# Weight splits moved up behind the joints, residual updates put ahead of them, two modulation tiles moved, and one scan matrix for both directions, in a two-layer hybrid trunk

## The chip, the cores and the metric

The kernel runs on one core of a Trainium2 chip (trn2). The metric is the device time of one execution in microseconds. The profile shows five engines: PE (TensorE, with its weight loads as PEld), DVE (VectorE), ACT (ScalarE), POOL (GpSimd) and SP (SyncE, which here only issues the weight transfers).

## What is computed

Two layers run over 384 tokens (256 latent, 128 context) with a model width of 1024, all in fp32. Cut to what matters here:

```python
h = rmsnorm(x, g1) * (1 + sc1) + sh1          # sc, sh, g: x @ w_mod rows of silu(c), silu(c_ctx)
u, q, k, v, z, xbc, dt_raw = split(h @ w_in)
o_pool = multiscale_pool_mixer(u)             # windows 2, 4, 8, 16
o_att  = diff_attention(rope(q), rope(k), v)  # 4 heads, two softmax maps each
xbc = silu(dwconv3(xbc)); dt = softplus(dt_raw + bias); a = -exp(A_log)
# per chunk of 128 tokens, head h, direction d (forward and backward):
#   y += (C B^T * exp(segsum_d) * dt_d) x  +  C (state_d * exp(cumsum_d))
o_ssd = rmsnorm_grouped((y_f + y_b + D * x) * silu(z))
merged = sum(sigmoid(h @ w_gate) * (o @ w_branch)) over the three branches
x = x + g1 * (merged @ w_out)
h2 = rmsnorm(x, g2) * (1 + sc2) + sh2
up = dwconv3(h2 @ w_up); x = x + g2 * ((silu(up_gate) * up_val) @ w_down)
```

The outputs are the two token streams after a last norm, the new keys and values, and the final scan states.

## The kernel before

**Units.** All dense products run as a list of units (`UNITS`), 140 to a layer, in this order: XBC 8, U 4, Q 4, K 4, V 4, Z 4, GATE 24, BRANCH 12, OUT 8, UP 44, DOWN 24. A unit is one 128x1024 block of weights (896 columns for some of DOWN). Its product is taken in three fp32r parts (high by high, high by low, low by high), so a unit is 24 matmuls of 128x384. Activations lie transposed, channels on partitions and tokens in the free dimension.

**Splits.** Weights come from HBM by SP into `raw` (4 slots). ACT copies the high part into `wh` (function `hi`, L1158), DVE takes the low part `wl` (function `lo`, L1511). Both have three slots, so unit u+3 can be split only when PE has finished unit u. The function `ahead(l, u)` of ACT and of DVE issues the split of unit u+3. In the loop over the units each engine does, for unit u: the bank's evacuation or taps, then `ahead`, then the rest (`conv_result`, `update` and others).

**Joints.** After each norm the first three units (XBC 0 to 2, or UP 0 to 2) run together (`joint`): for each of the eight tiles k of the normed input, PE multiplies with all three weight blocks as soon as `hh` and `hl` of that tile are there. For tiles 6 and 7 it waits for the last low part and then runs unit by unit.

**XBC and UP units.** They carry a depthwise convolution: ACT evacuates the bank with the middle tap (L1279), DVE adds the two outer taps in four instructions (L1661), ACT takes a tanh (L1317), DVE multiplies (`conv_result`, L1672, L1676, L1682). After each pair of UP units ACT and DVE write the product's high and low part (`ah` L1175, `al` L1516).

**OUT and DOWN units.** DVE adds the result to `x` (`update`, L1723), ACT squares the new `x` into `th` (L1261), POOL sums six of the squares into `sqa`. After the last unit, PE sums over channels (`mean_squares`, L774 to L778: first `sqa`, then the squares of tiles 6 and 7), ACT makes 1/rms, and the next norm begins.

**Modulation tiles.** The adaLN rows are computed on DVE beside the units, one tile of 128 weight rows at a place (`modulation`, L1586, two instructions of 128x1024). `mod_places` sets the places: in each layer every unit from U 0 to V 3 (`FRONT`), eight units of GATE, and every fifth of UP. Q 0 and K 0 also hold a rotation (L1691 to L1694).

**The scan** runs beside GATE and BRANCH, in six steps (chunk c of 3, group g of 2), one every two units. PE broadcasts the exponents (`rows`, L1056), DVE adds the column's part `nac` and a mask for each direction and head (`decays`, L1785), ACT takes the exponent (L1399, L1400), DVE multiplies by dt and by B^T C (`matrices`, L1796) and scales the entering states' factors `eb` (L1800), PE multiplies (`scan_out`, L1078). An fp32 matmul shows as two records.

## Time and profile before

| | |
|---|---|
| median of 3 runs | 1368.4 us (1368.32 to 1369.77) |
| the profiled execution's own time | 1367.94 us |
| its span, first to last instruction | 1366.2 us |
| PE busy | 1308.7 us, 96% |
| DVE busy | 1095.0 us, 80% |
| ACT busy | 647.9 us, 47% |
| POOL busy | 162.3 us, 12% |

Busy time of PE is the union of matmul records, whose ends are modelled; two records of neighbouring matmuls overlap. So for PE the distance between starts tells more than the busy share. A value in square brackets is idle time just before an instruction, with what ended it.

### The profile page before, as it was taken

The page shows a single profiled execution, that of the slowest core. Times are in us where ns is not written, and L with a number is a line of the kernel's source. Part 1 is how long each engine was busy: PE and PEld are TensorE (multiplying, and loading weights), DVE is VectorE, ACT ScalarE, POOL GpSimd, SP SyncE. Part 2 cuts the span into 40 slices and gives each one's busy share as a digit, 9 for nine tenths or more (in the row PEclk, how much of TensorE's full clock was granted, in tenths as well). Part 3 has the DMA queues.
Part 4 walks back from the last instruction along what each step waited for, and adds up shares of the span by engine and source line. Part 5 has one row for each costly group of instructions (what it writes and reads, how often), then busy time and mean ns, then how long its engine had stood idle before and what let it go on. Part 6 is the DMA issues. An engine that isn't in the chain of part 4 may idle for free.

```text
span 1366.2 us, 20140 instructions
## 1 busy us (share of the span) xinstructions
PE 1308.7 (96%) x7564; PEld 1245.6 (91%) x7564; DVE 1095.0 (80%) x2104; ACT 647.9 (47%) x1037; POOL 162.3 (12%) x167
## 2 busy tenths in 40 slices
PE   5899999999998999999999999999999899999996
PEld 4799889999997999999989978899999799999996
DVE  5889988779857999999958998877876689999432
ACT  4643445644546445442355335545455654454331
POOL 0058000000310000000102910000031000000001
PEclk8999999999999999999999999999999999999998
DMA  9466525433343444457725672552234254444441
GB/s 365 144 204 211 199 96 205 141 101 95 116 145 106 140 156 155 139 185 259 245 85 171 215 232 77 185 186 94 92 108 148 83 167 154 140 158 133 142 127 47
DMA packets 58433, 210.00 MB, mean 154 GB/s; under 512 B 6752, under 2 KB 8928, under 8 KB 56800
## 3 DMA queue, kind: packets, MB, share of 16 engines
q1 hardware_dynamic: 55648, 197.53, 43.6%
q0 software_dynamic: 2688, 11.18, 2.4%
q8 instruction: 60, 0.98, 0.3%
q14 instruction: 37, 0.30, 0.1%
HBM read 205.01 MB, written 3.67 MB: 153 GB/s over the span
## 4 chain that ended last, share of the span: by engine, by line
PE 60%; DVE 26%; ACT 7%; issue 5%; DMA 1%; POOL 0%; SPq 0%; ACTq 0%; DVEq 0%; POOLq 0%
PE acc L826 17%; PE acc L827 17%; PE acc L828 17%; DVE wl L1511 6%; DVE junk_front L1586 5%; DVE cv L1661 3%; ACT wh L1158 1%; DVE gates L1705 1%; PE mix L1078 1%; DVE ee L1796 1%; DVE ee L1785 1%; PE mix L983 1%; DMA head<-in_whead_dram 1%; DVE hl L1516 1%; DVE x L1723 1%
## 5 line engine op out<-in xcount | busy, mean ns | idle before, releaser
L826 PE MATMUL acc<-hh,wh 128*128 128x384 f32 x1528 | 522.2, 342 | 7.5 <-DVE wl L1511 5.3
L828 PE MATMUL acc<-hh,wl 128*128 128x384 f32 x1528 | 511.1, 334 | 0.0
L827 PE MATMUL acc<-hl,wh 128*128 128x384 f32 x1528 | 510.8, 334 | 0.0
L1511 DVE TENSOR_TENSOR wl<-raw,wh 128x1024 fp32r<-128x1024 f32 (+1 forms) x280 | 344.9, 1232 | 118.3 <-ACT wh L1158 116.5
L1158 ACT ACTIVATE wh<-raw 128x1024 fp32r<-128x1024 f32 (+1 forms) x280 | 291.1, 1040 | 128.7 <-PE acc L828 127.7
L826 PEld LDWEIGHTS acc<-hh,wh 128*128 128x128 f32 x1528 | 286.8, 188 | 23.7 <-DVE wl L1511 10.2
L827 PEld LDWEIGHTS acc<-hl,wh 128*128 128x128 f32 x1528 | 287.0, 188 | 2.3
L828 PEld LDWEIGHTS acc<-hh,wl 128*128 128x128 f32 x1528 | 286.8, 188 | 0.0
L1661 DVE SCALAR_TENSOR_TENSOR cv<-acc,prm,cv 128x1 f32<-128x1 f32 (+1 forms) x416 | 153.8, 412 | 11.2 <-ACT cv L1279 4.2
L828 PE MATMUL acc<-ah,wl 128*128 128x384 f32 x352 | 117.6, 334 | 0.0
L826 PE MATMUL acc<-ah,wh 128*128 128x384 f32 x352 | 117.6, 334 | 0.0
L827 PE MATMUL acc<-al,wh 128*128 128x384 f32 x352 | 117.6, 334 | 0.0
L1586 DVE SCALAR_TENSOR_TENSOR junk_front<-rawm,crow 128x1024 f32<-128x1024 f32 x64 | 87.4, 1401 | 0.0
L1175 ACT ACTIVATE ah<-cv 128x384 fp32r<-128x384 f32 x44 | 23.1, 525 | 132.5 <-DVE cv L1682 132.5
L1586 DVE SCALAR_TENSOR_TENSOR junk_ffn<-rawm,crow 128x1024 f32<-128x1024 f32 x64 | 78.4, 1263 | 0.0
L1279 ACT ACTIVATE cv<-acc,prm 128x384 f32<-128x384 f32 x104 | 68.3, 657 | 5.6 <-PE acc L828 5.6
L826 PEld LDWEIGHTS acc<-ah,wh 128*128 128x128 f32 x352 | 66.1, 188 | 0.0
L827 PEld LDWEIGHTS acc<-al,wh 128*128 128x128 f32 x352 | 66.1, 188 | 0.0
L828 PEld LDWEIGHTS acc<-ah,wl 128*128 128x128 f32 x352 | 66.1, 188 | 0.0
L1305 ACT ACTIVATE gates<-acc,bgh 128x384 f32<-128x384 f32 x48 | 27.9, 581 | 79.2 <-PE acc L828 79.2
L1317 ACT ACTIVATE th<-cv 128x384 f32<-128x384 f32 x60 | 31.6, 526 | 67.2 <-DVE cv L1661 67.2
L826 PE MATMUL acc<-mh,wh 128*128 128x384 f32 x128 | 43.0, 336 | 3.1 <-DVE ml L1516 3.1
(256 smaller groups left out, 1673.0 us busy)
## 6 DMA issues: line engine op xcount, KB each, us to landing
raw<-in_wstream_dram SPq DMA_DIRECT2D x248, 512.0 KB, 3.5
rawm<-in_wstream_dram SPq DMA_DIRECT2D x80, 512.0 KB, 3.8
raw<-in_wstream_dram SPq DMA_DIRECT2D x32, 448.0 KB, 3.4
head<-in_whead_dram SPq DMA_DIRECT2D x8, 1024.0 KB, 14.0
crow_late<-in_cvec_rows_dram POOLq DMA_DIRECT2D x2, 1024.0 KB, 6.6
crow<-in_cvec_rows_dram POOLq DMA_DIRECT2D x2, 1024.0 KB, 5.2
out_y_dram<-gates POOLq DMA_DIRECT2D x8, 192.0 KB, 2.6
prm<-in_par_dram POOLq DMA_DIRECT2D x2, 591.5 KB, 5.0
```

The source lines that it names most:

```text
L826: mm(out, sh, mhi, start=start, stop=False)
L827: mm(out, sh, mlo, start=False, stop=False)
L828: return mm(out, sl, mhi, start=False, stop=stop)
L983: last = mm(bank[:, 0:nk], qt[q, h, CHUNK0[t]:CHUNK0[t] + P], kt_[q, h, k0:k0 + nk], start=True, stop=True)
L1158: af(wh[:, s, 0:n], raw[:, raw_slot(u), 0:n], ACT.Copy).then_inc(hi_done, 1)
L1175: af(dst, src, ACT.Copy).then_inc(h_hi, 1)
L1279: af(cv[:, b_, :], bank[:, 0:T], ACT.Identity, bias=prm_(b, tile), scale=prm_(w, 3 * tile + 1)) \
L1305: af(gates[:, j, :], bank[:, 0:T], ACT.Tanh, bias=bgh[:, j:j + 1], scale=0.5).then_inc(g_done, 1)
L1317: af(th[:, b_, :], cv[:, b_, :], ACT.Tanh).then_inc(cv_tanh, 1)
L1511: tt(wl[:, s, 0:n], raw[:, raw_slot(u), 0:n], wh[:, s, 0:n].bitcast(F32), ALU.subtract).then_inc(lo_done, 1)
L1586: last = stt(out=junk[:, v, :], in0=rawm[:, n % NMOD, :], scalar=1.0, in1=rows[:, v, :], op0=ALU.mult, op1=ALU.mult, accum_out=macc[:, m, ...
L1661: return stt(out=out, in0=src, scalar=prm_(w, 3 * tile + i), in1=out, op0=ALU.mult, op1=ALU.add)
```

## The change

It has five parts. (1) In the joint, the splits of units 3, 4 and 5 are issued one iteration earlier: units 3 and 4 in the iteration of unit 0, unit 5 in that of unit 1. PE also takes tile 6 of the first unit, and the two products of tile 7 that need only its high part, before it waits for the last low part. (2) The modulation tiles of units Q 0 and K 0 move to XBC units 3 and 6. (3) In OUT, and in the last third of each DOWN product, DVE updates `x` before it issues the split; in the last BRANCH unit it writes the low parts of `merged` before the split. (4) In the scan, log dt goes into the exponent (`exponents`), so one matrix is the sum of the two directions' and is multiplied by B^T C once; PE has one product with it where it had two. (5) log dt is a new small activation at the end of the attention norm, on dt floored at 1e-37.

```diff
--- before.py
+++ after.py
@@ -96,10 +97,23 @@
     LO_NUMBER[_u] = _u % NU in POOL_LO, _n[_u % NU in POOL_LO]
 
 FRONT = range(UU0, MIX0)
+ROTATED = (U_OF[(QQ, 0, 0)], U_OF[(KK, 0, 0)])
+EARLY = (3, 6)
 LATE_ROWS = MIX0 + 9
 LATE = range(LATE_ROWS, LATE_ROWS + 8)
 LATE_DONE = LATE[-1]
 LATE_TILE = 13
+
+
+def joint_place(u):
+
+    return next((u - u0 for u0 in (0, UP0) if u0 <= u < u0 + JOINT), None)
+
+
+def updates(u):
+
+    kind, _j, part = UNITS[u]
+    return kind == OUT or kind == DOWN and part == 2
 
 
 def closing_unit(g):
@@ -130,7 +144,7 @@
     tiles = [(l, m) for l in range(DEPTH) for m in range(MODT)][MOD_HEAD:]
     units = []
     for l in range(DEPTH):
-        units += [(l, u) for u in FRONT] + [(l, u) for u in LATE]
+        units += [(l, u) for u in EARLY] + [(l, u) for u in FRONT if u not in ROTATED] + [(l, u) for u in LATE]
         units += [(l, UP0 + 5 * i + 4) for i in range(MODT - MOD_G2)]
         if l + 1 < DEPTH:
             units += [(l, DOWN0 + i) for i in range(MOD_HEAD + 2) if i not in (8, 17)]
@@ -924,8 +940,15 @@
                     pe.wait_ge(h_lo, count(l, NSPLIT, split0 + k))
                     for i in range(JOINT):
                         mm(banks[i][:, 0:T], weights(i, k)[0], hl[:, k, :], start=False, stop=False)
+                pe.wait_ge(h_lo, count(l, NSPLIT, split0 + KT - 2))
+                product(0, KT - 2)
+                pe.wait_ge(h_hi, count(l, NSPLIT, split0 + KT - 1))
+                w1, w2 = weights(0, KT - 1)
+                mm(banks[0][:, 0:T], w1, hh[:, KT - 1, :], start=False, stop=False)
+                mm(banks[0][:, 0:T], w2, hh[:, KT - 1, :], start=False, stop=False)
                 pe.wait_ge(h_lo, count(l, NSPLIT, split0 + KT - 1))
-                for i in range(JOINT):
+                mm(banks[0][:, 0:T], w1, hl[:, KT - 1, :], start=False, stop=True).then_inc(unit_used, 1)
+                for i in range(1, JOINT):
                     product(i, KT - 2)
                     product(i, KT - 1).then_inc(unit_used, 1)
 
@@ -1070,7 +1093,7 @@
                     out = mix7[64 * (i % 2):64 * (i % 2) + 64, P * (i // 2):P * (i // 2) + P]
                     hs = slice(SSD_P * h, SSD_P * h + SSD_P)
                     ms = slice(P * i, P * i + P)
-                    terms = [(xt[:, c, hs], ee[:, d, ms]) for d in range(2)]
+                    terms = [(xt[:, c, hs], ee[:, 0, ms])]
                     if c < 2:
 
                         terms += [(hst[:, (0, 3)[d] if c == 0 else (2, 1)[d], hs], eb[:, d, ms]) for d in range(2)]
@@ -1373,6 +1396,8 @@
                     h = s - SLOT_A
                     if h == HEADS - 1:
                         act.preload_act_table_set(LN_EXP)
+                        act.wait_ge(dt_floor, l + 1)
+                        af(dte[:, :], dte[:, :], ACT.Ln).then_inc(ln_done, 1)
                     act.wait_ge(misc_done, count(l, NMISC, M_ATT + h))
                     af(rst[:, h, :], mz, ACT.Copy).then_inc(att_ss, 1)
                     if h == HEADS - 1:
@@ -1452,13 +1477,15 @@
                     if UNITS[u] in ((OUT, 4, 0), (DOWN, 4, 2)):
 
                         act.preload_act_table_set(LN_EXP)
-                    if u in (0, UP0):
+                    if joint_place(u) == 0:
                         ahead(l, u)
                     done = done_after(u)
                     for g in done:
                         if GROUPS[g][0] in (XBC, UU, QQ, KK, VV, ZZ, GATE, UP):
                             evac(l, g)
-                    if u not in (0, UP0):
+                    if joint_place(u) in (0, 1):
+                        ahead(l, u + 1)
+                    if joint_place(u) is None:
                         ahead(l, u)
                     for g in done:
                         kind, j = GROUPS[g]
@@ -1789,16 +1816,13 @@
             def matrices(l, y_):
                 c, g = divmod(y_, 2)
                 dve.wait_ge(e_done, count(l, NY, y_))
-                for d in range(2):
-                    for i in range(4):
-                        col = 16 * c + SSD_H * d + 4 * g + i
-                        m_ = ee[:, d, P * i:P * i + P]
-                        last = stt(out=m_, in0=m_, scalar=dtt[:, col:col + 1], in1=bg[:, c, P * (2 + g):P * (3 + g)],
-                                   op0=ALU.mult, op1=ALU.mult)
-                    if c < 2:
-                        e3 = eb[:, d, :].rearrange("p (i t) -> p i t", i=4)
-                        last = tt(e3, e3, xbc[:, 6 + g, CHUNK0[c]:CHUNK0[c] + P].unsqueeze(1).to_broadcast([P, 4, P]),
-                                  ALU.mult)
+                step.then(tt(ee[:, 0, :], ee[:, 0, :], ee[:, 1, :], ALU.add))
+                m3 = ee[:, 0, :].rearrange("p (i t) -> p i t", i=4)
+                last = tt(m3, m3, bg[:, c, P * (2 + g):P * (3 + g)].unsqueeze(1).to_broadcast([P, 4, P]), ALU.mult)
+                for d in range(2 if c < 2 else 0):
+                    e3 = eb[:, d, :].rearrange("p (i t) -> p i t", i=4)
+                    last = tt(e3, e3, xbc[:, 6 + g, CHUNK0[c]:CHUNK0[c] + P].unsqueeze(1).to_broadcast([P, 4, P]),
+                              ALU.mult)
                 last.then_inc(m_done, 1)
 
             def gate_z(l, y_):
@@ -1847,6 +1871,7 @@
                 if SLOT_S - 1 <= s < SLOT_S + 3:
                     weighted(l, s - SLOT_S + 1)
                 if s == SLOT_A + HEADS:
+                    exponents(l)
                     dve.wait_ge(ors_done, l + 1)
                     for h in range(HEADS):
                         last = stt(out=ot[:, h, :], in0=ot[:, h, :], scalar=sg[:, 0:1], in1=rst[:, h, :], op0=ALU.mult,
@@ -1864,9 +1889,17 @@
                 stt(out=bd[0:96, i, :], in0=csh_[0:96, :].bitcast(F32), scalar=heads[0:96, i:i + 1],
                     in1=bd[0:96, i, :].bitcast(F32), op0=ALU.mult, op1=ALU.add).then_inc(bd_done, 1)
 
+            def exponents(l):
+
+                dve.wait_ge(ln_done, l + 1)
+                for d in range(2):
+                    last = tt(nac[:, 24 * d:24 * d + 24].rearrange("p (c h) -> p c h", c=NCH),
+                              dte[:, :].rearrange("p (c h) -> p c h", c=NCH)[:, :, SSD_H * d:SSD_H * d + SSD_H],
+                              sm[:, 24 * d:24 * d + 24].rearrange("p (c h) -> p c h", c=NCH), ALU.subtract)
+                step.then(last)
+
             def chunk_weights(l):
 
-                ts(nac[:, :], sm[:, 0:48], -1.0, None, ALU.mult)
                 dve.wait_ge(ede_done, l + 1)
                 for d in range(2):
                     last = tt(wdc[:, 24 * d:24 * d + 24].rearrange("p (c h) -> p c h", c=NCH),
@@ -1884,6 +1917,7 @@
 
                     dve.wait_ge(dt_log, l + 1)
                     step.then(stt(out=dtt[:, :], in0=dtv[:, :], scalar=0.0, in1=dte[:, :], op0=ALU.max, op1=ALU.add))
+                    ts(dte[:, :], dtt[:, :], TINY, None, ALU.max).then_inc(dt_floor, 1)
                     stt(out=adt[:, :].rearrange("p (c h) -> p c h", c=NCH), in0=dtt[:, :].rearrange("p (c h) -> p c h", c=NCH),
                         scalar=-1.0, in1=eal[:, :].unsqueeze(1).to_broadcast([P, NCH, 16]), op0=ALU.mult,
                         op1=ALU.mult).then_inc(adt_done, 1)
@@ -1952,7 +1986,7 @@
 
                         summed(l + 1, 0, MOD_HEAD)
                         scale_of(sc1, norm1_weight(l + 1), KT).then_inc(scale_ready, 1)
-                    if u in (0, UP0):
+                    if joint_place(u) == 0:
                         ahead(l, u)
                     done = done_after(u)
                     for g in done:
@@ -1963,8 +1997,10 @@
                             branch(l, g)
                     if MIX0 <= u <= MIX0 + SLOT_RMS + 1:
                         mixers_a(l, u - MIX0)
-                    last_update = UNITS[u] in ((OUT, KT - 1, 0), (DOWN, KT - 1, 2))
-                    if u not in (0, UP0) and not last_update:
+                    last_merged = UNITS[u] == (BRANCH, 3 * KT - 2, 0)
+                    if joint_place(u) in (0, 1):
+                        ahead(l, u + 1)
+                    if joint_place(u) is None and not updates(u) and not last_merged:
                         ahead(l, u)
                     for g in done:
                         kind, j = GROUPS[g]
@@ -1985,7 +2021,7 @@
                         low(l, SP_MG + jj, ml[:, jj, :], cv[:, jj % 2, :], mh[:, jj, :])
                     if MIX0 <= u <= MIX0 + SLOT_RMS + 1:
                         mixers_b(l, u - MIX0)
-                    if last_update:
+                    if updates(u) or last_merged:
                         ahead(l, u)
                     if u == LATE_ROWS - 1:
                         rows_silu(2 * l + 1, crow_late, junk_late)
```

How this moves instructions, at three places. First, DVE at the start of XBC in layer 0, after `params`, before the change (`wl` is a split, L1661 are taps, L1672 is `conv_result`):

```order
L1511 TENSOR_TENSOR wl<-raw,wh 128x1024
L1661 SCALAR_TENSOR_TENSOR cv<-acc,prm,cv 128x1
L1661 SCALAR_TENSOR_TENSOR cv<-acc,prm,cv 128x3x127
L1661 SCALAR_TENSOR_TENSOR cv<-acc,prm,cv 128x1
L1661 SCALAR_TENSOR_TENSOR cv<-acc,prm,cv 128x3x127
L1672 SCALAR_TENSOR_TENSOR xbc<-th,cv 128x384
L1661 SCALAR_TENSOR_TENSOR cv<-acc,prm,cv 128x1
L1661 SCALAR_TENSOR_TENSOR cv<-acc,prm,cv 128x3x127
L1661 SCALAR_TENSOR_TENSOR cv<-acc,prm,cv 128x1
L1661 SCALAR_TENSOR_TENSOR cv<-acc,prm,cv 128x3x127
L1511 TENSOR_TENSOR wl<-raw,wh 128x1024
```

The same stretch of the changed kernel:

```order
L1538 TENSOR_TENSOR wl<-raw,wh 128x1024
L1688 SCALAR_TENSOR_TENSOR cv<-acc,prm,cv 128x1
L1688 SCALAR_TENSOR_TENSOR cv<-acc,prm,cv 128x3x127
L1688 SCALAR_TENSOR_TENSOR cv<-acc,prm,cv 128x1
L1688 SCALAR_TENSOR_TENSOR cv<-acc,prm,cv 128x3x127
L1538 TENSOR_TENSOR wl<-raw,wh 128x1024
L1699 SCALAR_TENSOR_TENSOR xbc<-th,cv 128x384
```

The split of unit 4 stands five instructions earlier, ahead of unit 0's `conv_result`; that of unit 5 moves ahead of unit 1's in the same way, and unit 2 has none. The UP joint reads alike, with L1676 and L1682 for L1672.

Second, DVE in one scan step of a chunk with entering states, before the change, from `decays` to the next split:

```order
L1785 SCALAR_TENSOR_TENSOR ee<-mix,nac,tb 128x128 x8
L1511 TENSOR_TENSOR wl<-raw,wh 128x1024
L1796 SCALAR_TENSOR_TENSOR ee<-ee,dtt,bg 128x128 x4
L1800 TENSOR_TENSOR eb<-eb,xbc 128x512
L1796 SCALAR_TENSOR_TENSOR ee<-ee,dtt,bg 128x128 x4
L1800 TENSOR_TENSOR eb<-eb,xbc 128x512
```

and in the changed kernel:

```order
L1812 SCALAR_TENSOR_TENSOR ee<-mix,nac,tb 128x128 x8
L1538 TENSOR_TENSOR wl<-raw,wh 128x1024
L1819 TENSOR_TENSOR ee<-ee 128x512
L1821 TENSOR_TENSOR ee<-ee,bg 128x512
L1824 TENSOR_TENSOR eb<-eb,xbc 128x512 x2
L1538 TENSOR_TENSOR wl<-raw,wh 128x1024
```

Eight products of 128x128 have become one sum and one product of 128x512. PE has one matmul with `ee` for each head where it had two.

Third, DVE from the last BRANCH unit into OUT, before the change:

```order
L1705 SCALAR_TENSOR_TENSOR gates<-gates,acc 128x384
L1714 TENSOR_TENSOR cv<-gates 128x384
L1511 TENSOR_TENSOR wl<-raw,wh 128x1024
L1516 TENSOR_TENSOR ml<-cv,mh 128x384 x2
L1511 TENSOR_TENSOR wl<-raw,wh 128x1024
L1723 SCALAR_TENSOR_TENSOR x<-acc,g1h,x 128x256
L1723 SCALAR_TENSOR_TENSOR x<-acc,g1h,x 128x128
```

and in the changed kernel:

```order
L1732 SCALAR_TENSOR_TENSOR gates<-gates,acc 128x384
L1741 TENSOR_TENSOR cv<-gates 128x384
L1543 TENSOR_TENSOR ml<-cv,mh 128x384 x2
L1538 TENSOR_TENSOR wl<-raw,wh 128x1024
L1750 SCALAR_TENSOR_TENSOR x<-acc,g1h,x 128x256
L1750 SCALAR_TENSOR_TENSOR x<-acc,g1h,x 128x128
L1538 TENSOR_TENSOR wl<-raw,wh 128x1024
```

The split now follows the low parts of `merged`, and in each OUT unit it follows the update.

## Rows read from the trace of the kernel before

**Rows 1.** Waits of PE: what waited for what, total us, times, longest.

```profile
PE acc L826 <- DVE wl L1511: 7.7, 10, 1.2
...
PE acc L826 <- DVE ml L1516: 3.1, 2, 1.6
```

**Rows 2.** Stretches: busy us (count) of PE, PEld, DVE, ACT, POOL; granted clock, DMA.

```profile
415.20:422.00 6.80, 6.80 (x39) 6.80 (x40) 5.70 (x13) 6.67 (x16) 0.00 (x0) 1.00 0.07 28
...
697.50:704.20 6.70, 5.75 (x18) 5.79 (x19) 6.01 (x14) 6.58 (x15) 0.00 (x0) 0.50 0.18 63
...
480.00:520.00 40.00, 40.00 (x233) 40.00 (x232) 36.33 (x72) 19.10 (x28) 0.00 (x0) 1.00 0.47 148
```

**Rows 3.** Timeline, end of layer 0's UP joint: start, us, engine, instruction, [idle].

```profile
424.97 0.45 PE L826 MATMUL acc<-hh,wh 128*128 128x384 f32 x1 [0.21 <-DVE hl L1516]
...
426.38 1.06 ACT L1158 ACTIVATE wh<-raw 128x1024 fp32r<-128x1024 f32 x1 [0.76 <-PE acc L828]
...
427.48 1.23 DVE L1511 TENSOR_TENSOR wl<-raw,wh 128x1024 fp32r<-128x1024 f32 x1 [2.56 <-ACT wh L1158]
...
430.72 0.56 DVE L1676 SCALAR_TENSOR_TENSOR th<-th,cv 128x384 f32<-128x384 f32 x1 [0.59 <-ACT th L1317]
...
438.72 1.51 DVE L1661 SCALAR_TENSOR_TENSOR cv<-acc,prm,cv 128x1 f32<-128x1 f32 x4
```

**Rows 4.** Timeline of DVE and PE, further into UP.

```profile
452.84 1.52 DVE L1661 SCALAR_TENSOR_TENSOR cv<-acc,prm,cv 128x1 f32<-128x1 f32 x4
...
460.21 1.51 DVE L1661 SCALAR_TENSOR_TENSOR cv<-acc,prm,cv 128x1 f32<-128x1 f32 x4
...
471.26 1.22 DVE L1511 TENSOR_TENSOR wl<-raw,wh 128x1024 fp32r<-128x1024 f32 x1
...
472.53 0.45 PE L826 MATMUL acc<-hh,wh 128*128 128x384 f32 x1
```

**Rows 5.** Timeline of PE, XBC units 3 and 4 of layer 1.

```profile
714.27 0.45 PE L826 MATMUL acc<-hh,wh 128*128 128x384 f32 x1 [0.41 <-DVE wl L1511]
...
719.56 0.44 PE L826 MATMUL acc<-hh,wh 128*128 128x384 f32 x1 [0.86 <-DVE wl L1511]
```

**Rows 6.** Timeline of layer 0: Q 0's tile and its split, then V 0.

```profile
103.72 1.48 DVE L1586 SCALAR_TENSOR_TENSOR junk_front<-rawm,crow 128x1024 f32<-128x1024 f32 x1
...
107.07 1.77 DVE L1511 TENSOR_TENSOR wl<-raw,wh 128x1024 fp32r<-128x1024 f32 x1
...
128.87 0.50 PE L826 MATMUL acc<-wh,hh 128*128 128x512 f32 x1 [1.16 <-DVE wl L1511]
```

**Rows 7.** Timeline of layer 0's scan steps, PE and DVE.

```profile
274.32 1.14 DVE L1796 SCALAR_TENSOR_TENSOR ee<-ee,dtt,bg 128x128 f32<-128x128 f32 x4 [1.03 <-ACT ee L1400]
...
277.03 0.68 DVE L1800 TENSOR_TENSOR eb<-eb,xbc 128x512 f32<-128x512 f32 x1
...
277.77 0.65 PE L1078 MATMUL mix<-ee,xt 128*64 128x128 f32 x4 [0.74 <-DVE eb L1800]
...
280.27 0.49 PE L1056 MATMUL mix<-bd,selr 32*128 32x512 f32 x1
...
335.05 1.15 PE L1078 MATMUL mix<-ee,xt 128*64 128x128 f32 x16 [0.17 <-DVE ee L1796]
```

**Rows 8.** Timeline of PE, from the last OUT matmul to the UP joint, layer 0.

```profile
408.27 0.34 PE L828 MATMUL acc<-mh,wl 128*128 128x384 f32 x1
...
410.75 0.91 PE L776 MATMUL misc<-th,tb 128*128 128x384 f32 x2 [1.34 <-ACT th L1261]
...
415.16 0.41 PE L922 MATMUL acc<-hh,wh 128*128 128x384 f32 x1 [2.74 <-ACT hh L1224]
```

**Rows 9.** Timeline of PE, from the last DOWN matmul of layer 0 into layer 1.

```profile
692.95 0.34 PE L828 MATMUL acc<-ah,wl 128*128 128x384 f32 x1
...
694.79 0.91 PE L778 MATMUL misc<-th,tb 128*128 128x384 f32 x2 [0.21 <-DVE th L1730]
...
698.45 0.66 PE L922 MATMUL acc<-hh,wh 128*128 128x384 f32 x1 [2.74 <-ACT hh L1224]
```

3 lines of the change are left out of this document (added).

## The prediction

> **What bounds the kernel now.** I read the table of the page first: PE is busy 96% of the span, DVE 80%, so time can only come from what PE does or waits for. Then the waits of PE [rows 1]: it waits 7.7 us in all for a weight split (`wl`) and 3.1 us for the low part of `merged`. Then the stretches [rows 2]: where nothing disturbs it PE starts 233 matmuls in 40 us, one each 0.172 us, so a unit of 24 takes about 4.15 us. The distance between starts shows what a wait costs: XBC 3 starts at 714.27 and XBC 4 at 719.56 [rows 5], 5.29 us for one unit. The bracket says 0.86; the rest, 0.28, is drain (the first matmul can't overlap the last one) and a slow first step. So a short wait costs its bracket and about 0.3. Last the timelines, stage by stage, since DVE sets the pace in some and PE in others.
>
> **XBC (both layers).** Unit 4 waited because its split stood behind unit 0's `conv_result` and unit 1's taps. Now it stands in front of them: from the split of unit 3 to that of unit 4 there is one set of taps (1.5 us), not two. That removes the 0.86 and its 0.3, about 1.15 a layer, and another 0.1 at unit 5. Against it stand the tiles moved to units 3 and 6. DVE does in one XBC unit taps 1.5, split 1.2 and a product 0.5, 3.2 of the 4.15 us, so it makes good 1 us a unit; a tile costs it 2.4 there. Counting on from the split of unit 3, the split of unit 7 ends within 0.2 us of PE's need. I charge 0.2 in layer 1: 1.25 and 1.05 us gained.
>
> **Front (Q 0, K 0).** DVE works without a stop from Q 0 to the mixers. Q 0's tile holds it from 103.72 to 107.07, 3.35 us [rows 6], where the next split waits behind it; K 0's costs 2.4 or more. PE then waits 1.16 for V 0's split. With both tiles gone DVE is over 4 us ahead at V 0, so the wait goes with its 0.3, and 0.3 of small waits behind it: 1.75 a layer. Lag left over from XBC (at most 1.5 us) is covered by those 4. If that cover were gone, the 1.16 would come back.
>
> **Scan.** Of the scan's matmuls PE does sixteen fp32 ones, 32 records, in a step with entering states, from 277.77 to 280.27 [rows 7]: 2.50 us, 0.078 a record. Four matmuls (eight records) go: 0.62 a step in four steps. In the two steps without states 16 records take 1.07 us, from the same group's last row (1.15 less the overlap of its end), so eight less is 0.53. That is 3.5 us a layer of PE's own work, in a stage where PE has hardly a bracket. DVE's part: `matrices` ran from 274.32 to 277.71 (277.03 and 0.68) [rows 7], 3.4 us. Of that the two products with `eb` stay, 1.3 us. The new sum and product have the shape of `eb`'s (0.68, or 0.6 back to back), so 1.3 us where there were 2.1; in all 2.6. `exponents` adds two operations of 128x24 before the first step, some 0.35 with its semaphore, once a layer. So PE's first wait, 0.74, falls by 0.8 - 0.35 = 0.45, and the 0.17 of the last step goes. Sum 4.1 a layer. The new logarithm (128x48 on ACT, well below the 0.5 of its 128x384 kinds) lies beside DVE's weighting of the states, which has to end first.
>
> **End of BRANCH.** PE stops in OUT 0 for the low part of `merged`, 3.1 us in two stops, 1.57 each [rows 1]. The split in front of it (1.14 back to back) moves behind. The gain is 1.1 a layer: then ACT's high part of the last tile is what PE waits for.
>
> **OUT to UP.** Here the skipped wait is on ACT. The square of tile 6 came late (bracket 1.34) because ACT's square waited for an update that stood behind a split, so from the last OUT matmul to the UP joint it is 408.27 to 415.16, 6.89 us [rows 8]. The same passage after DOWN, where squares were in time, is 692.95 to 698.45, 5.50 us [rows 9]. The update now comes first; I take the whole difference, 1.4 a layer. DOWN gains nothing by it, as [rows 9] show. In OUT the split ends about 0.8 later after its unit, but three units ahead of need, so that costs nothing; without that lead it would cost 0.8 a unit.
>
> **UP.** Here I don't believe the brackets. DVE and ACT pass the taps, the tanh and the products back and forth, and two units take them 452.84 to 460.21, 7.37 us [rows 4]. The next split but one, behind a modulation tile, starts at 471.26: 11.05 after 460.21, that is 7.37, taps of 1.45 and a tile of 2.2. Ten units with two tiles make 41.3 us; PE needs 240 x 0.172 = 41.3. And PE starts UP 13 at 472.53, 0.05 after that split's end. So what UP gains is what this loop gains, not what PE no longer waits at units 3 to 5. How much is that? The loop starts with the split of UP 3, at 426.38 on ACT, which waited 0.76 for PE [rows 3]. PE had waited 0.21 at 424.97 for the last low part and restarted slowly; with tile 6 done beforehand unit 0 ends 0.48 earlier, and ACT's table load allows that. From the split at 427.48 to unit 3's taps at 438.72 the instructions are the same before and after. The new order fills the 0.59 that DVE waited for unit 0's tanh, but leaves nothing to do during unit 2's tanh (0.53 and the two handovers, 0.65). So the stretch stays as long, and the gain is 0.45 a layer, with a new wait of over 1 us at UP 8, where PE, ahead of the loop, meets it again.
>
> **Sum.** A layer: 1.15 + 1.75 + 4.1 + 1.1 + 1.4 + 0.45 = 9.95 us; both 19.9. The profiled execution's own time is 1367.94, the median of the runs 0.46 more.
>
> **The clock.** The passages between OUT or DOWN and a joint don't all end alike. After 698.45 the granted clock is 0.50 (1.2 GHz), and 18 matmuls start in 6.7 us; after 415.16 it is 1.00 (2.4 GHz), with 39 in 6.8 [rows 2]. Before the first, PE had run its sums right behind the unit and then stood idle 2.74 us; before the second, one sum came late, and then the same 2.74 [rows 8, 9]. The first joint took 714.27 - 698.45 = 15.8 us to unit 3. The UP joint, its split at 427.48 + 1.23, took 13.5, and 13.05 after the change. So a stretch at half clock costs 2.7 us. After the change all three passages have the form of the one that fell. I take one more fall as likeliest: +2.7. The Trainium skill ("TensorE: Matmul & The Clock Gate", section "HAM oscillation — how this bites in real kernels") says that a long enough pause between bursts puts the clock back and the next burst starts cold, which speaks against a change that makes these pauses alike. The trace agrees in one passage of three; by the rule as a rival, all three fall.
>
> So: 1367.94 - 19.9 + 2.7 = 1350.7, and 0.46 more for the median: **1351.2 us**.
>
> **Rivals.**
> - No further fall, or none at all: 1348.5 or 1345.8. For it: the UP joints run at 1.00 now, after a longer passage. Against it: the sums now end sooner, as before 698.45.
> - All three joints at half clock: 1353.9.
> - UP gives its brackets back in full. XBC-like, 0.39 and 0.83 with their 0.3 at units 3 and 4, and about 1 us of small waits later, some 2.8 a layer instead of 0.45: 1351.2 - 4.7 = 1346.5. For it: the waits are there. Against it: [rows 4].
> - The scan becomes DVE's. PE now comes back 0.62 earlier each step; if the two 512-wide operations took as long as the eight they replace (2.1 us, nothing here shows the in-place sum), PE would wait for `matrices` in most steps, and the 3.5 falls to about 1: 1356.2. It decides once they take over about 1.9 us together.
> - Slower: the UP loop settles in another rhythm. If the 0.65 that unit 2 now waits for its tanh recurred in every pair (22 a layer), 44 x 0.65 = 28.6 us would be added where the loop already is the bound: 1379.8. It decides at 0.38 us a pair (16.7 / 44). Against it: from unit 3 on the order is unchanged, and the split lies between taps and product as before.
> - That the change does nothing would need PE's removed matmuls to be hidden; they have neither gap nor parallel work on PE.
>
> **How the numbers follow.** Chances: one more fall 0.37; none or one fewer 0.22; three in all 0.18; UP in full 0.10; scan held by DVE 0.09; slower 0.02; the small rest for edits that cancel without my seeing it. The forecast's own range, with the terms of XBC and front unsure by 1 us and `exponents` and the passage by 1 each, is 1349 to 1353.5. The range for 8 in 10 takes in the clock cases and part of the scan's: 1345.5 to 1356. What the measurement can tell from no change is 0.2%, 2.7 us. Faster 0.96, same 0.01, slower 0.03.
>
> **What would show it.** In the changed trace: no wait at XBC 4, V 0, and under 0.3 in OUT 0; 24 and 8 records in the scan's steps, of 1.9 and 0.5 us; 5.5 us from OUT to the UP joint; a wait of 1 us or so at UP 8, and UP 3 to the end of UP only 0.45 better; a granted clock of 0.50 in two of the three joints. It is wrong if UP's waits vanish, if PE waits for `ee` in each scan step, or if the clock stays up.

## The result, and the profile after

The changed kernel takes **1349.0 us** (median of four executions, 1348.22 to 1350.48) where the kernel before took 1368.9 (1368.32 to 1369.77). The ratio is 0.985, with an interval of 0.9834 to 0.9865. The profiled execution took 1348.22 us with a span of 1346.2, so 20.0 us of span are gone. One later execution, of the kernel without UP's tiles, took 1391.06 us at a mean granted clock of 0.938 and is left out of that run's figures. I forecast 1351.2, in a range of 1345.5 to 1356.

The page's first table:

```profile
PE 1298.7 (96%) x7468; PEld 1237.8 (92%) x7468; DVE 1089.0 (81%) x2036; ACT 646.5 (48%) x1039; POOL 175.6 (13%) x167
```

PE is busy 10.0 us less, DVE 6.0 less. The waits of PE (total us, times, longest), which answer to [rows 1]:

```profile
PE acc L938 <- ACT hh L1247: 8.2, 3, 2.7
PE acc L842 <- DVE wl L1538: 5.0, 7, 1.5
...
PE acc L842 <- DVE ml L1543: 0.9, 2, 0.4
```

Splits are waited for seven times and no longer ten, and the low part of `merged` for 0.44 us instead of 1.57. The list doesn't show waits too short for it, nor drain and slow restarts. So I measured each unit by the distance from its first matmul to the next unit's in both traces (4.16 us where nothing disturbs it; below, the unit distance). The sum of the differences is 20.0 us, the whole change of the span:

| place | layer 0, us gained | layer 1 | forecast a layer |
|---|---|---|---|
| XBC 0 to 7 | 1.13 | 0.87 | 1.25 and 1.05 |
| K 3, V 0, V 1, Z 1 | 2.07 | 1.76 | 1.75 |
| scan (GATE 17 to BRANCH 6) | 4.36 | 4.33 | 4.1 |
| OUT 0 | 0.97 | 0.99 | 1.1 |
| OUT 7 (joint into UP) | 1.40 | 1.40 | 1.4 |
| UP | 0.51 | 0.24 | 0.45 |
| clock | 0 | 0 | -2.7 in all |

**XBC and front.** Timeline of PE (start, us, engine, line, instruction, idle before), at XBC 3 and XBC 4 of layer 1, then at V 0 of layer 0:

```profile
703.89 0.44 PE L842 MATMUL acc<-hh,wh 128*128 128x384 f32 x1 [0.41 <-DVE wl L1538]
...
708.17 0.33 PE L842 MATMUL acc<-hh,wh 128*128 128x384 f32 x1
```

```profile
126.16 0.33 PE L844 MATMUL acc<-hh,wl 128*128 128x384 f32 x1
126.33 0.39 PE L842 MATMUL acc<-wh,hh 128*128 128x512 f32 x1
```

XBC 3 to XBC 4 is 4.28 us where [rows 5] have 5.29. The 0.41 ahead of XBC 3 is as before. V 0 starts 0.17 after the last matmul of K 3, without the 1.16 of [rows 6].

**Scan.** First the two engines in layer 0's first step. DVE's matrices, then PE's products from 274.05, the next step's broadcast at 275.78 and the next unit. Below them the same for a step without states, and DVE's new `exponents` in the view of lines:

```profile
271.37 0.69 DVE L1819 TENSOR_TENSOR ee<-ee 128x512 f32<-128x512 f32 x1 [1.03 <-ACT ee L1425]
...
272.10 0.69 DVE L1821 TENSOR_TENSOR ee<-ee,bg 128x512 f32<-128x512 f32 x1
...
272.71 1.29 DVE L1824 TENSOR_TENSOR eb<-eb,xbc 128x512 f32<-128x512 f32 x2
...
274.05 0.43 PE L1101 MATMUL mix<-ee,xt 128*64 128x128 f32 x2 [0.28 <-DVE eb L1824]
...
275.78 0.72 PE L1079 MATMUL mix<-bd,selr 32*128 32x512 f32 x2
...
327.86 0.66 PE L1101 MATMUL mix<-ee,xt 128*64 128x128 f32 x8
328.45 0.44 PE L842 MATMUL acc<-hh,wh 128*128 128x384 f32 x1
```

```profile
L1896 DVE TENSOR_TENSOR nac<-dte,sm 128x24 f32<-128x24 f32 x2 | 0.3, 176 | 0.0
```

`matrices` takes 271.37 to 274.00, 2.63 us (2.6 forecast). PE's products take 1.73 us where they took 2.50 [rows 7], a step without states 0.59 to the next unit where it took 1.08. The wait ahead of the first is 0.28, not 0.74. The logarithm's part, `exponents`, takes 0.3 us once. The fourth step with states gains only 0.37, though its products too are 0.78 shorter, since a wait stands behind it that had been covered. It is the low part of the normed input (`hl`), before BRANCH 0:

```profile
308.50 0.72 PE L1079 MATMUL mix<-bd,selr 32*128 32x512 f32 x2
309.56 0.41 PE L842 MATMUL acc<-hh,wh 128*128 128x384 f32 x1 [0.33 <-DVE hl L1543]
```

**OUT to UP.** Timeline of PE: `merged` in OUT 0, the last matmul of OUT, the last sum, and the joint.

```profile
369.42 0.44 PE L842 MATMUL acc<-mh,wh 128*128 128x384 f32 x1 [0.44 <-DVE ml L1543]
...
399.68 0.34 PE L844 MATMUL acc<-mh,wl 128*128 128x384 f32 x1
...
401.51 0.91 PE L794 MATMUL misc<-th,tb 128*128 128x384 f32 x2 [0.20 <-DVE th L1757]
405.17 0.41 PE L938 MATMUL acc<-hh,wh 128*128 128x384 f32 x1 [2.75 <-ACT hh L1247]
```

The passage is 5.49 us (6.89 in [rows 8], 5.50 forecast). It now has the form of the passage in [rows 9]: 0.20, then 2.75.

**UP.** Timeline, PE's last matmul of UP 7 and its first of UP 8; DVE's modulation tile, and UP 8's split behind the tile and a set of taps:

```profile
439.38 0.34 PE L844 MATMUL acc<-hh,wl 128*128 128x384 f32 x1
440.73 0.45 PE L842 MATMUL acc<-hh,wh 128*128 128x384 f32 x1 [1.01 <-DVE wl L1538]
```

```profile
435.62 1.22 DVE L1613 SCALAR_TENSOR_TENSOR junk_ffn<-rawm,crow 128x1024 f32<-128x1024 f32 x1
...
438.02 1.52 DVE L1688 SCALAR_TENSOR_TENSOR cv<-acc,prm,cv 128x1 f32<-128x1 f32 x4
439.46 1.22 DVE L1538 TENSOR_TENSOR wl<-raw,wh 128x1024 fp32r<-128x1024 f32 x1
```

UP gains 1.7 us at its first units and pays 1.1 back at UP 8, as the prediction's loop says.

**The clock.** Stretches around the joint into UP of layer 0, the joint into XBC of layer 1 and the joint into UP of layer 1 (busy us and count of PE, PEld, DVE, ACT, POOL; granted clock; DMA), as [rows 2]:

```profile
403.40:409.40 6.00, 4.23 (x24) 4.26 (x25) 5.49 (x13) 5.31 (x13) 0.00 (x0) 1.00 0.27 90
687.20:694.00 6.80, 6.04 (x19) 6.07 (x20) 5.99 (x14) 6.67 (x16) 0.00 (x0) 0.50 0.10 40
...
1052.00:1059.00 7.00, 4.92 (x28) 4.95 (x29) 5.77 (x14) 6.28 (x15) 0.00 (x0) 1.00 0.21 75
```

Only the joint that ran at half clock before does so again. Both UP joints follow a pause of the same 2.75 us and stay at 1.00. In this execution the forecast's +2.7 did not come.

### The profile page after: what moved, and what is told of

Read it like the earlier page. It is cut to its first block, busy times and chain, and to the rows that moved or that the text cites. A ratio compares the mean times of both kernels' runs of the same rounds, so it can differ in the third digit from the quotient of the medians.

```text
span 1346.2 us, 19880 instructions
## 1 busy us (share of the span) xinstructions
PE 1298.7 (96%) x7468; PEld 1237.8 (92%) x7468; DVE 1089.0 (81%) x2036; ACT 646.5 (48%) x1039; POOL 175.6 (13%) x167
## 4 chain that ended last, share of the span: by engine, by line
PE 68%; DVE 20%; issue 4%; ACT 4%; DMA 2%; POOL 0%; SPq 0%; ACTq 0%; DVEq 0%; POOLq 0%
PE acc L842 20%; PE acc L844 19%; PE acc L843 19%; DVE wl L1538 4%; DVE cv L1688 3%; DVE junk_front L1613 3%; DVE gates L1732 1%; DMA crow_late<-in_cvec_rows_dram 1%; PE acc L938 1%; DVE ee L1812 1%; PE acc L939 1%; PE acc L942 1%; PE mix L1006 1%; DMA head<-in_whead_dram 1%; PE mix L1101 1%
## 5 line engine op out<-in xcount | busy, mean ns | idle before, releaser
L842 PEld LDWEIGHTS acc<-hh,wh 128*128 128x128 f32 x1524 | 286.1, 188 | 20.9 <-DVE wl L1538 9.2
L653 POOL TENSOR_TENSOR sqa<-sqa,th 128x384 f32<-128x384 f32 x20 | 29.5, 1476 | 127.6 <-ACT th L1284 127.6
```

The source lines that it names most:

```text
L653: nc.gpsimd.tensor_tensor(sqa[:, :], sqa[:, :], th[:, j % 2, :], ALU.add).then_inc(sq_sum, 1)
L842: mm(out, sh, mhi, start=start, stop=False)
```

## The experiments

Four take one part of the change each, on the kernel before. Four alter one thing in the changed kernel. The last four ask about the clock and combine what helped. The kernel before ran beside them, with 1368.9 us for the first four, 1368.6 for the next and 1369.5 for the last. A ratio is the recorded one against these runs; it is not the quotient of the two medians, and lies up to 0.0008 below it. The code shown is a cut of each edit.

### Each part alone

**Part 1, splits and joint.**

```diff
-                    if u not in (0, UP0):
+                    if joint_place(u) in (0, 1):
+                        ahead(l, u + 1)
+                    if joint_place(u) is None:
                         ahead(l, u)
...
```

> The kernel before with the first part alone: behind the joints UP and XBC the splits of units 1 to 5 move up by one unit, and PE starts the joint's last product apart. Mine (each part adds its own term): the waits at XBC 3 and 4 and at UP 3 and 4 go (1.14 + 0.13 us each time, of which the records of the changed kernel gave back 1.1 at XBC and lost as much to a new wait of 1.28 us before UP 8), so 2 x 1.3 for XBC and 2 x 0.45 for UP, 1368.9 - 3.4 = 1365.5 us; a wait of about 1 us stands at UP 8. Rival (the UP part is not held by DVE and ACT, and its wait at UP 8 in the changed kernel came from another part of the change): the UP joints give 1.3 each too, 1363.8 us and no wait at UP 8.

Measured: 1365.8 us (twelve executions, 1362.83 to 1368.79), ratio 0.9977 (0.9967 to 0.9988). The wait at UP 8 is there with nothing else changed:

```profile
447.29 0.34 PE L833 MATMUL acc<-hh,wl 128*128 128x384 f32 x1
448.62 0.44 PE L831 MATMUL acc<-hh,wh 128*128 128x384 f32 x1 [1.00 <-DVE wl L1525]
```

No other part of the change is needed to make it. By the unit distances, leaving out a half clock in one UP joint, UP gives 0.51 a layer and XBC 3 and 4 give 1.15.

**Part 2, tiles.**

```diff
-        units += [(l, u) for u in FRONT] + [(l, u) for u in LATE]
+        units += [(l, u) for u in EARLY] + [(l, u) for u in FRONT if u not in ROTATED] + [(l, u) for u in LATE]
```

> The kernel before with the second part alone: the modulation tiles leave Q 0 and K 0 for XBC 3 and 6. Mine: the waits before V 0 and in Q and K go, 1.32 + 0.45 = 1.75 us per layer as measured between the two kernels, and XBC 3 and 6 can lose some of it, since here their splits still come a unit later: between 0.3 and 0 us per layer. Together -3.5 us, 1365.4, at most 1366.0. Rival: the tiles at XBC lengthen the wait at XBC 4 (0.13 us before) by the length of a tile on DVE, so that half of the gain or more is lost: 1367 us or above.

Measured: 1364.3 us, ratio 0.9965 (0.9953 to 0.9977). K 3, V 0, V 1 give 1.55 a layer and Z 1 gives 0.51, 4.1 us in all; XBC pays nothing. The rival falls.

This trace also bears on the clock. Nothing here touches the passage from OUT to UP, which keeps the late sum of [rows 8]. Yet both UP joints ran at half clock (the joint of layer 0 starts at 413.11), and the joint into XBC of layer 1 did not: it took 13.62 us where it took 15.82 before.

```profile
412.80:416.20 3.40, 3.09 (x10) 3.12 (x11) 3.40 (x9) 3.34 (x9) 0.00 (x0) 0.50 0.24 92
692.00:699.00 7.00, 4.05 (x18) 2.58 (x17) 5.64 (x12) 4.74 (x10) 0.27 (x3) 1.00 0.41 146
```

**Part 3, updates.**

```diff
-                    if u not in (0, UP0) and not last_update:
+                    if u not in (0, UP0) and not updates(u) and not last_merged:
                         ahead(l, u)
...
```

> The kernel before with the third part alone: in OUT and in the last third of DOWN the update stands in front of the splits. Mine: the wait at OUT 0 and the waits of the branches just ahead fall by 1.1 us, and the OUT to UP joint by 1.4 us, per layer, together -5.0 us, 1363.9 us, and DOWN to XBC gives nothing. Rival (the gain at OUT belongs to the scan, which leaves DVE earlier, and not to the order in OUT): 0 at OUT 0 and 1.4 at the joint, -2.8 us, 1366.1 us.

Measured: 1364.7 us, ratio 0.9969 (0.9958 to 0.998). OUT 0 gives 0.98 and OUT 7 gives 1.40 in each layer, 4.8 us. Here the wait for `merged` is already down to what the whole change has, so the gain at OUT 0 is not the scan's:

```profile
376.53 0.45 PE L832 MATMUL acc<-mh,wh 128*128 128x384 f32 x1 [0.43 <-DVE ml L1522]
```

**Part 4 and 5, one matrix.**

```diff
-                    terms = [(xt[:, c, hs], ee[:, d, ms]) for d in range(2)]
+                    terms = [(xt[:, c, hs], ee[:, 0, ms])]
...
-                        last = stt(out=m_, in0=m_, scalar=dtt[:, col:col + 1], in1=bg[:, c, P * (2 + g):P * (3 + g)],
-                                   op0=ALU.mult, op1=ALU.mult)
...
+                step.then(tt(ee[:, 0, :], ee[:, 0, :], ee[:, 1, :], ALU.add))
+                m3 = ee[:, 0, :].rearrange("p (i t) -> p i t", i=4)
+                last = tt(m3, m3, bg[:, c, P * (2 + g):P * (3 + g)].unsqueeze(1).to_broadcast([P, 4, P]), ALU.mult)
...
```

> The kernel before with the fourth part alone: one matrix for both directions in the scan, with the exponent of dt in it, 9 PE products fewer in each of the six pairs of a scan step and DVE work merged. Mine: 1.24 + 2 x 0.77 + 0.37 at the scan's steps, 0.5 before it, and something of 0.5 to 1.2 us in the branches behind it: 4.2 us per layer, -8.4 us, 1360.5 us. Rival (the waits that the changed kernel loses in the branches and at OUT 0 all come from a scan that ends earlier on DVE, not from the updates' new place): 5.3 us per layer or more, 1358.3 us. If the four parts add up, the sum of the four gains is 20 us; if parts share a wait it is more than 20, and if one part needs another it is less.

Each scan step loses four matmuls, eight records, and not nine products. Measured: 1358.2 us, ratio 0.9928 (0.9914 to 0.9941). The median is what the rival said. Yet the records deny its mechanism, for OUT 0 has its whole wait:

```profile
374.87 0.45 PE L842 MATMUL acc<-mh,wh 128*128 128x384 f32 x1 [1.56 <-DVE ml L1534]
```

The unit distances give 4.4 us in layer 1. In layer 0 they give 3.3, since in this execution DVE waited 2.71 us in one step for the transfer that reads `cv`, a buffer which DVE writes next, and PE at GATE 19 then waited 0.97 for DVE. Without this single wait, which the later run of the same part doesn't have, the scan is worth 4.4 a layer, 8.7 in all. That left 2 us between median and records open, and I come back to it below.

Added up, the parts' unit distances are 3.3 + 4.1 + 4.8 + 8.7 = 20.9 us without stretches of half clock and that wait, and the whole change has 20.0. The parts barely touch each other. What is missing lies in the first joint and XBC 7 (0.13 a layer), at UP 12 of layer 1 (0.26) and in Z 1 of layer 1 (0.29). The last is no interplay of parts: DVE waited 0.91 us there for a tile's rows to arrive, and in the second execution of the changed kernel, where it doesn't, Z 1 is 0.29 shorter.

### What holds UP

**No DVE work for UP's modulation tiles.**

```diff
+                if UP0 <= u < DOWN0:
+                    nc.vector.memset(macc[:, m, :], 0.0).then_inc(mod_used, 1)
+                    dve.wait_ge(mod_used, n + 1)
+                    return
```

The kernel leaves these eight tiles out, so the second half's gate (`g2`) is not computed and the outputs are not the reference's. PE's work and the other instructions of DVE stay.

> The changed kernel without the DVE work of the eight modulation tiles in UP of each layer (a memset of one column stands for it, so the modulation of the second half is left out of the result). Mine: UP is held by the loop of DVE and ACT (7.37 us per pair of units plus a tile of 2.2 us in five units), so without the tiles the wait of 1.28 us before UP 8 and the small ones behind it (0.2 us) go, 1.3 to 1.6 us per layer, -2.9 us, 1346.1 us. Rival (the wait before UP 8 is the debt of the joint alone, DVE late by a fixed amount whatever the tiles): the wait stays, 1349.0 us.

Measured: 1344.7 us (median of four executions, 1343.70 to 1346.84), ratio 0.982 (0.98 to 0.9841). PE from UP 7 to UP 8, first matmul of each:

```profile
436.98 0.44 PE L842 MATMUL acc<-hh,wh 128*128 128x384 f32 x1
...
441.27 0.33 PE L842 MATMUL acc<-hh,wh 128*128 128x384 f32 x1
```

The distance is 4.29 us where the changed kernel has 5.44, and the small waits at UP 8 to 13 are gone too: 1.8 us in layer 0, 2.1 in layer 1. So the loop of DVE and ACT, with its tile, holds UP's first ten units, and a wait that were the joint's debt alone would have stayed. The tile is the part of the load which can be moved.

**UP 5's split back in its old place.**

```diff
-                    if joint_place(u) in (0, 1):
+                    if joint_place(u) == 0 or u == 1:
                         ahead(l, u + 1)
+                    if u == UP0 + 2:
+                        ahead(l, u)
```

> The changed kernel, but in UP the splits of unit 5 go back to their place of before (a unit later than now), XBC as changed. Mine: what delays UP 8 is one pair of splits more ahead of the evictions of the first units, so the wait before UP 8 (1.28 us) falls by about 0.65 us per layer and nothing comes back at UP 5 or 6: -1.3 us, 1347.7 us. Rival (the loop of DVE and ACT sets UP's end whatever the order): the wait moves to UP 6 or 7 with the same sum, 1349.0 us.

Measured: 1348.45 us, ratio 0.9845 (0.9821 to 0.9869), not to be told from the changed kernel; the profiled execution had half clock at all three joints. The unit distances, which leave that out, side with my expectation and against the rival: 0.65 and 0.61 a layer are gained. UP 7 is 1.08 shorter, UP 4 pays 0.53, and UP 5 and 6 nearly even out. So the order of the splits matters to the loop, and moving UP 5's forward cost the change 1.3 us.

**Three of UP's eight tiles moved to OUT 3 to 5.**

```diff
-        units += [(l, UP0 + 5 * i + 4) for i in range(MODT - MOD_G2)]
+        units += [(l, OUT0 + 3 + i) for i in range(3)]
+        units += [(l, UP0 + 8 * i + 7) for i in range(MODT - MOD_G2 - 3)]
...
```

> The changed kernel with three of the eight modulation tiles of UP moved to OUT 3 to 5, where DVE has room, and the other five spread, one in eight units, the first at UP 7. Mine: in the first ten units of UP there is one tile in the place of two, so the wait before UP 8 of 1.28 us and those of 0.26 and 0.2 us behind it go almost whole, 1.3 us per layer, and OUT pays nothing: -2.6 us, 1346.4 us. Rival (OUT has no room, as the evictions and updates wait for DVE there): waits of 0.5 us or more stand at OUT 6 or 7 per layer, 1348.5 us or above.

Measured: 1351.35 us, ratio 0.9869 (0.9849 to 0.9889), slower than the changed kernel by 2.3 us. The wait at UP 8 did go, and UP is 1.4 and 1.7 us shorter behind its joint, but the passage from OUT to the joint grew by 2.5 and 2.1 us. DVE in OUT (two updates at a time, a split, the tile's two instructions), then PE's last sums and the joint:

```profile
395.04 0.74 DVE L1751 SCALAR_TENSOR_TENSOR x<-acc,g1h,x 128x256 f32<-128x256 f32 x2
395.70 1.21 DVE L1539 TENSOR_TENSOR wl<-raw,wh 128x1024 fp32r<-128x1024 f32 x1
396.83 2.03 DVE L1614 SCALAR_TENSOR_TENSOR junk_front<-rawm,crow 128x1024 f32<-128x1024 f32 x1
...
398.80 1.21 DVE L1614 SCALAR_TENSOR_TENSOR junk_front<-rawm,crow 128x1024 f32<-128x1024 f32 x1
...
400.06 0.74 DVE L1751 SCALAR_TENSOR_TENSOR x<-acc,g1h,x 128x256 f32<-128x256 f32 x2
```

```profile
401.41 0.91 PE L793 MATMUL misc<-th,tb 128*128 128x384 f32 x2 [1.02 <-ACT th L1285]
403.30 1.35 PE L795 MATMUL misc<-th,tb 128*128 128x384 f32 x2 [0.98 <-DVE th L1758]
407.39 0.66 PE L939 MATMUL acc<-hh,wh 128*128 128x384 f32 x1 [2.75 <-ACT hh L1248]
```

DVE's round is 395.04 to 400.06, 5.02 us, against PE's 4.16. Three rounds leave 2.6 us, which the squares of the last tiles show as waits of 1.02 and 0.98. I expected room for three and there is room for fewer. The two UP joints of this execution also ran at half clock (0.66 instead of 0.41 for the first matmul), and took 1.4 and 2.5 us longer for it, which adds to its time but not to the waits above. By the unit distances without the clock the moved tiles cost 1.4 us; the rest of the 2.3 between the medians may be the clock's.

The round is longer than I had worked out because a tile's first instruction takes 2.03 us here, and 1.22 in UP. POOL's add of a square lies beside it:

```profile
396.42 1.36 POOL L654 TENSOR_TENSOR sqa<-sqa,th 128x384 f32<-128x384 f32 x1 [3.66 <-ACT th L1285]
```

It ends at 397.78, 0.95 us after the tile's first instruction began, and that instruction is 0.81 longer than without company; the second, at 398.80, is not. The same is seen in the other two rounds of this layer (2.03 and 2.04).

### The clock

**Three more products in each pause.** Their result goes to a bank that is free there and is read by nobody.

```diff
+                at = TAB["cos"][0]
+                for _ in range(3 if n < 2 * DEPTH - 1 else 0):
+                    mm(mix6[:, 0:T], ones, tb[:, at:at + T], start=True, stop=True)
```

> The changed kernel with three more products behind the sums of each norm, into a bank that is free there, so that PE isn't idle in the joint's pause. Mine: the granted clock stays at full in the joints; where the joint into XBC of layer 1 ran at half clock its first unit took 2.8 us more than a full clock gives, and a wait behind it of 0.5 us took part of that back, so the gain is 2.2 to 2.7 us against an execution with that one fall, more where an execution has falls at UP too (about 1 us each in the kernels with one part): 1346.6 us. Rival (the fall is not set by the pause of PE, or the extra products delay the first product of the joint): half clock at XBC again, 1349.0 to 1350 us.

Measured: **1344.7 us** (1344.13 to 1344.99), ratio 0.9817 (0.9798 to 0.9837). The joint into XBC of layer 1 in the timeline, and its stretch:

```profile
684.51 2.10 PE L797 MATMUL mix<-tb 128*128 128x384 f32 x6
687.42 0.41 PE L941 MATMUL acc<-hh,wh 128*128 128x384 f32 x1 [0.81 <-ACT hh L1250]
```

```profile
684.00:694.00 10.00, 9.19 (x46) 7.81 (x46) 7.86 (x17) 8.51 (x19) 0.00 (x0) 1.00 0.18 54
```

The last sum starts 3.66 us ahead of the joint, as without the products (684.30 and 687.96 there), so they delay nothing. The joint takes 13.13 us, 2.8 less than in the first trace of the changed kernel. The spans of the two traces differ by 3.7 us: besides this joint by 0.3 at Z 1 of layer 1 (the late rows above) and by 0.5 at the kernel's start. The medians differ by 4.4, so other executions of the changed kernel may have had more falls. With the pause filled, PE keeps its clock at these joints.

**The kernel before with the same products.** Only the lines above were added to it.

> The kernel before, with the three products more behind the sums of each norm and nothing else. If the whole change is worth the sum of its waits, the difference to the changed kernel with the same products (1344.7 us) is 20.0 us whatever the clock does: 1364.7 us. Rival (the clock's falls took part of the gain in the changed kernel, or gave it some): below 1363.5 or above 1366 us. The joint into XBC of layer 1 had half clock before too, at a price of 2.2 us, so at most 1366.5 us in any case.

Measured: 1365.75 us (1365.21 to 1366.47), ratio 0.9967 (0.9955 to 0.9979). Its joint into XBC of layer 1 is 2.2 us shorter: 2.66 in its first 24 matmuls, less 0.45 in its last 24, where PE now waits for the last low part, as at UP [rows 3]. The two kernels are 21.1 us apart with the products and 19.9 without, by medians from rounds whose kernels before differ by 0.9. The unit distances show 0.6 of this at the joint: at full clock the change is worth so much more. Half clock had hidden the wait for the last low part there, which part 1 takes away.

**The scan's part alone, with the products.** The kernel of part 4 and 5, with the same lines added.

> The kernel with the scan's part alone, with the three products more. Its records showed 4.37 us per layer less waiting in gates and branches, its median 10.7 us less time. Mine (the median owes the rest to the clock, which fell in another number of joints in its executions than in those of before): 8.7 us below the kernel before with the same products, 1356.0 us if that one takes 1364.7 us. Rival (the scan's part saves something that the records of one execution don't show): 10.7 us below, 1354.0 us.

Measured: 1357.4 us (1356.88 to 1360.14), ratio 0.9909 (0.9893 to 0.9924). It is 8.4 us below its base, near the 8.7 of the records, and not 10.7. The highest execution is the profiled one, and it has a fall of the clock in Z of layer 1, where no products were added, behind a wait of 1.36 us:

```profile
811.51 0.55 PE L1016 MATMUL mix<-tb,pr 128*128 128x128 f32 x3 [1.36 <-DVE pr L1769]
```

```profile
814.00:817.40 3.40, 3.40 (x13) 3.40 (x12) 3.23 (x10) 1.24 (x4) 0.00 (x0) 0.50 0.20 39
```

By the unit distances the fall cost 1.6 us, in Z 2. The longer wait before it cost another 1.05, in Z 1, and isn't the clock's: DVE had waited 0.53 and 0.35 us for tiles' rows. Part 3's trace has 1.49 us at the same place, behind a wait of DVE of 1.11 for such rows, and no fall.

The 2 us that the median of the scan's part had too much are within what the clock does between executions. The mean granted clock, which every execution has, points the same way. It was 0.988 in the profiled execution of part 4 and 5 (1362.4 us, three falls) and 0.990 to 0.992 in four of its other five (1357.0 to 1358.2), where the kernel before had 0.986 to 0.990. Which joints fell in those that weren't profiled isn't known, since the mean takes in the kernel's start and end too.

**The changed kernel once more.** Nothing is altered.

> The changed kernel once more, unaltered, beside the others. Its four executions so far took 1348.2 to 1350.5 us: the same, 1349 us, unless executions with falls of the clock at UP come up, which cost about 1 us each, so up to 1351 us.

Measured: 1349.9 us (1349.34 to 1350.38), ratio 0.9851 (0.9835 to 0.9866). The profiled execution took 1350.3 and has half clock at all three joints behind a norm, each time for half as long as in [rows 2]:

```profile
405.80:409.20 3.40, 3.40 (x13) 3.40 (x12) 3.12 (x8) 3.34 (x8) 0.00 (x0) 0.50 0.02 5
689.10:692.50 3.40, 3.13 (x10) 3.16 (x11) 3.40 (x9) 3.34 (x9) 0.00 (x0) 0.50 0.15 63
1054.40:1057.80 3.40, 3.40 (x13) 3.40 (x12) 3.12 (x9) 3.34 (x8) 0.00 (x0) 0.50 0.00 0
```

The two at UP add 1.61 and 1.57 us to their joints. The one at XBC is 1.33 cheaper than the long one. The span is 1347.5 us, only 1.3 more than in the first trace. The three pauses before the joints are the same as there. So the same program, with the same pauses, has one fall or three.

All profiled executions without the products, taken together, have 24 falls at 30 such joints, behind pauses of 2.74 or 2.75 us: one of three in the kernel before and in the first trace of the changed one, two of three with part 1 and with part 2, three of three in the other six. Where the last sum still came late, as in [rows 8], UP joints fell in five of eight cases. The four kernels with the products have none at twelve.

### Both together

**The products, and two tiles in OUT 4 and 5.**

```diff
-        units += [(l, UP0 + 5 * i + 4) for i in range(MODT - MOD_G2)]
+        units += [(l, OUT0 + 4 + i) for i in range(2)]
+        units += [(l, UP0 + 7 * i + 7) for i in range(MODT - MOD_G2 - 2)]
...
```

> The changed kernel with the three products more, and with two of UP's eight modulation tiles moved to OUT 4 and 5 and the other six one in seven units. Three tiles at OUT 3 to 5 made each OUT unit 5.03 us long on DVE against 4.16 us on PE, which came out as 2.2 us at the joint. Mine: two tiles leave 1.7 us of delay behind OUT 5, which OUT 6 (1.95 us of DVE work in 4.16 us) takes back, so the joint stays 5.3 us of waiting and UP loses its wait before UP 8: 1.3 us per layer, 1344.7 - 2.6 = 1342.1 us. Rival (the delay reaches OUT 7): 0.9 us per layer is paid at the joint, 1343.8 us.

Measured: **1342.6 us** (1341.78 to 1342.94), ratio 0.9797 (0.9782 to 0.9812), the lowest of all. It is 2.1 us below the products alone, by medians of two rounds. The joint pays 0.11 a layer:

```profile
402.55 0.91 PE L795 MATMUL misc<-th,tb 128*128 128x384 f32 x2 [0.31 <-DVE th L1761]
406.20 0.41 PE L942 MATMUL acc<-hh,wh 128*128 128x384 f32 x1 [0.81 <-ACT hh L1251]
```

UP 7 to UP 13 give 1.46 us in layer 0 and 1.72 in layer 1 by unit distances. Against that stand the two joints' 0.22 and 0.11 at GATE 6, and in the profiled executions a first matmul that came 1.3 us later at the kernel's start, which the edit doesn't touch.

## Why the prediction was right, and where it was not

- **The sum of the waits held.** 19.9 us were forecast without the clock, 20.0 came. No term was off by more than 0.35 us a layer. That the sums agree to 0.1 is luck: the differences of the single terms come to 1.6 us if all are counted as positive, and they cancel. OUT 0 keeps a wait of 0.44 where under 0.3 was named, and its term is 0.1 smaller for it.
- **UP held, against its brackets.** The claim that the loop of DVE and ACT, and not PE's waits at UP 3 to 5, decides was the boldest step. Part 1 alone made the wait at UP 8 (1.00 us), and without the tiles' work it was gone. What the prediction missed is that UP 5's earlier split is itself a loss: with it back in its place the loop gave 0.6 a layer more. The rival that UP gives its brackets in full (1346.5) needed 2.8 a layer, where 0.51 and 0.24 came. Layer 1's UP gives less because of 0.26 at UP 12. It is in both traces of the changed kernel and in that with the products: some 7.6 us before UP 12 starts DVE stops for 0.17 us inside a set of taps, waiting for nothing that the profile shows, and all that follows is late by it. The rival of a slower loop decides at 0.39 us a pair and not at 0.38, if the forecast median is taken from the median before.
- **Scan: sizes off, sum right.** A removed record was priced at the mean of the step, 0.078 us. But 24 records take 1.73 where 32 took 2.50, so the removed ones cost 0.096 each, and a step with states gains 0.77 and not 0.62. The new wait of 0.33 for `hl` before BRANCH 0, which the prediction didn't have, takes back 0.4. The rival that DVE holds the scan needed 1.9 us for the two 512-wide operations; they take 1.42 (271.37 to 272.79).
- **Front: undersized.** Z 1, two stages on, gives 0.51 more when tiles are moved alone. There PE had waited 0.29 us for DVE's `pr` and restarted slowly, since DVE works on without a stop until then. With DVE ahead, this wait is gone. XBC's drag from the tiles was charged 0.2, and 0.13 was there at XBC 7.
- **OUT to UP came out as forecast**, a passage of 5.49 us against 5.50, since it was read off the passage after DOWN, which had the form that the change gives.
- **The clock: the step that failed.** The step is "I take one more fall as likeliest: +2.7". It was wrong in two ways. First, the form of the passage, a sum late or in time, doesn't decide over a fall. Of the changed kernel's three passages with 2.75 us of pause one fell in one execution, and all three in another, and UP joints fell in five of eight cases where the passage kept its old form. Second, a fall has no one price. The 2.7 set XBC's 15.8 us before against UP's 13.05 after; the fall there cost 2.2 in the kernel before (13.61 with the products) and 2.8 in the changed one. A fall at UP in this kernel cost 1.6, as its half clock lasted 3.4 us. Three falls of the short kind gave 1350.3, not 1353.9. So it was chance that the first execution profiled had as many falls as the kernel before. The rule of the Trainium skill ("TensorE: Matmul & The Clock Gate", section "HAM oscillation — how this bites in real kernels"), that a long enough pause puts the clock back and the next burst starts cold, holds in the direction: with the pause filled, none of the twelve joints in four profiled executions fell. It does not tell whether one execution falls behind 2.75 us: 24 joints of 30 did. Another sentence of that page, in the section "What's actually happening", says that the count of slow matmuls varies from run to run with the phase at the kernel's start. The two traces of the changed kernel agree that it varies; that the phase is the cause no run here shows.

What stays open is why a joint falls in one execution and not in the next, and which executions have which falls. The median of the scan's part probably owed some 2 us to it. Only the profiled execution of each kernel shows where its clock fell; of the others the mean is known.
